# Small products of the identity between the first modulation chunks, the bias ahead of the sum, and a new order of six weight blocks

## What is computed

```python
def modulation(cond, w_mod, b_mod):
    m = jax.nn.silu(cond) @ w_mod + b_mod
    return jnp.split(m[..., None, :], 6, axis=-1)
...
    for l in range(DEPTH):
        mp = modulation(c_ctx, w_mod[l], b_mod[l])
        ms = modulation(c, w_mod[l], b_mod[l])
        hp = modulate(xp, mp[0], mp[1])
        hs = modulate(xs, ms[0], ms[1])
...
            op, ckv, kpe, kb, vb = ab_context(hp, w_in_ab[i], mla_q_norm[i], mla_w_uq[i], ...)
            os_ = ab_latent(hs, cache_mla_ckv[:, i], ...)
...
        xp = layer_norm(ALPHA * xp + mp[2] * op, ln_g[l, 0], ln_b[l, 0])
...
        fp = moe(hp, router_w, router_bias, exp_w_gate[l], exp_w_up[l], exp_w_down[l])
```

## Time and profile before

| | |
|---|---|
| median of 3 runs | 822.41 us (822.19 to 824.67) |
| the profiled execution's own time | 821.88 us |
| its span in the trace | 820.1 us |
| PE busy | 759.0 us (93% of the span) |
| DMA moved | 287.46 MB, 351 GB/s over the span |
| mean granted clock of TensorE | 0.977 |

### The profile page before, as it was taken

The page is one execution under the profiler, slowest core; times in us unless marked ns, Lnnn a source line. Parts: engine busy times, 40 slices in busy tenths (PEclk is TensorE's granted clock), DMA queues, the critical chain, the costliest instruction groups (busy, mean ns, idle before and its releaser), DMA issues.

```text
span 820.1 us, 9612 instructions
## 1 busy us (share of the span) xinstructions
PE 759.0 (93%) x3769; PEld 361.2 (44%) x3769; DVE 237.2 (29%) x550; ACT 150.9 (18%) x390; POOL 59.7 (7%) x116
## 2 busy tenths in 40 slices
PE   4799799999999999997999999999999999997894
PEld 1345444556544443443334564455544434442431
DVE  0002634447401101000418227374601010010417
ACT  0110312325011110111112132233211101110200
POOL 0000000000100010101000110000100002101000
PEclk9599999999999999999999999999999999999998
DMA  8999999915399999999999999752299999999981
GB/s 305 390 304 396 390 390 416 415 68 206 121 418 417 419 421 417 419 416 415 421 401 374 389 380 423 299 211 104 109 419 416 422 417 416 421 418 416 418 352 52
DMA packets 78530, 287.46 MB, mean 351 GB/s; under 512 B 6508, under 2 KB 12140, under 8 KB 62100
## 3 DMA queue, kind: packets, MB, share of 16 engines
q1 hardware_dynamic: 74452, 275.60, 84.9%
q10 hardware_dynamic: 2880, 7.03, 2.2%
q0 software_dynamic: 1152, 4.19, 1.3%
HBM read 278.99 MB, written 7.82 MB: 350 GB/s over the span
## 4 chain that ended last, share of the span: by engine, by line
PE 56%; SPq 23%; DMA 9%; DVE 8%; ACT 3%; issue 2%; POOL 0%; DVEq 0%; ACTq 0%
PE bank L1094 13%; SPq L600 12%; PE bank L1128 7%; DMA ring<-in_exp_w_down 6%; SPq L595 6%; PE bank L932 6%; PE bank L789 5%; PE bank L769 4%; SPq L596 4%; PE bank L1065 3%; DMA ring<-in_w_mod 2%; PE bank L878 2%; PE bank L671 2%; PE bank L720 2%; PE bank L820 2%
## 5 line engine op out<-in xcount | busy, mean ns | idle before, releaser
L1094 PE MATMUL bank<-ring,arena 128*64 128x512 f32 x1024 | 227.6, 600 | 11.3 <-DMA ring<-in_exp_w_up 10.5
L1094 PEld LDWEIGHTS bank<-ring,arena 128*64 128x64 f32 x1024 | 75.2, 138 | 160.3 <-issue 148.8
L1128 PE MATMUL bank<-ring,arena 128*64 128x512 f32 x512 | 114.3, 596 | 6.0 <-DMA ring<-in_exp_w_down 4.9
L1679 DVE TENSOR_TENSOR arena<-bank,arena 128x256 f32<-128x256 f32 x32 | 13.6, 424 | 231.5 <-ACT arena L1848 231.5
L1128 PEld LDWEIGHTS bank<-ring,arena 128*64 128x64 f32 x512 | 35.8, 137 | 72.7 <-issue 63.6
L1065 PE MATMUL bank<-arena 128*128 128x128 f32 x512 | 62.1, 275 | 0.0
L1065 PEld LDWEIGHTS bank<-arena 128*128 128x128 f32 x512 | 59.7, 192 | 1.0 <-issue 0.5
L1758 ACT ACTIVATE arena<-bank 128x512 f32<-128x512 f32 (+6 forms) x67 | 37.2, 579 | 107.6 <-PE bank L789 34.0
L1848 ACT ACTIVATE arena<-bank 128x256 f32<-128x256 f32 x32 | 12.3, 383 | 225.7 <-PE bank L1094 225.7
L1695 DVE COPY arena<-bank 128x512 f32<-128x512 f32 x14 | 9.7, 691 | 118.7 <-PE bank L1128 118.7
L789 PE MATMUL bank<-ring,arena 128*128 128x256 f32 (+1 forms) x128 | 41.6, 486 | 0.0
(11 more groups left out here) (182 smaller groups left out, 679.6 us busy)
## 6 DMA issues: line engine op xcount, KB each, us to landing
ring<-in_exp_w_gate SPq DMA_DIRECT2D x64, 1024.0 KB, 19.8
ring<-in_exp_w_up SPq DMA_DIRECT2D x64, 1024.0 KB, 19.6
ring<-in_exp_w_down SPq DMA_DIRECT2D x64, 1024.0 KB, 23.7
ring<-in_w_mod SPq DMA_DIRECT2D x24, 2048.0 KB, 19.8
expert_rows<-arena ACTq DMA_DIRECT2D x12, 512.0 KB, 7.9
ring<-in_w_out_ab SPq DMA_DIRECT2D x2, 2048.0 KB, 19.2
ring<-in_w_in_c SPq DMA_DIRECT2D x2, 2048.0 KB, 23.2
ring<-in_w_out_c SPq DMA_DIRECT2D x2, 2048.0 KB, 12.0
```

The costliest lines, as they stand in the source:

```text
L1094: mm = nc.tensor.matmul(pb(key)[SLOTS * hf:SLOTS * (hf + 1), :], xeT[b][:, k * P + SLOTS * a:k * P + SLOTS * (a + 1)], w[:, :, k % 4, hf * ...
L1128: mm = nc.tensor.matmul(pb(key)[SLOTS * a:SLOTS * (a + 1), :], hp[:, c:c + SLOTS], w[:, a, kf % 2, hf * HALF:(hf + 1) * HALF], start=(kf = ...
```

## The change

Four edits. First, ahead of the wait for each of the chunks 0 to 3, PE makes ten products of the 128 x 128 identity with itself (`stir`), into a bank that the next transposes use later. Second, in piece 0 the product with the bias comes ahead of the chunks and starts the sum. Third, both pieces are closed by a product with zeros that is two columns wide and not 512. Fourth, the order of six blocks changes from `wout 1, lora, 8, 9, 10, 11` to `8, 9, lora, wout 1, 10, 11`, and qa0 gets a wait for `lora` of its own.

```diff
--- before.py
+++ after.py
@@ -105,8 +105,9 @@
 def plan_blocks():
 
     order = [("mod", 0, c) for c in MOD_PIECES[0]] + [("win", 0, b) for b in range(3)]
-    order += [("mod", 0, c) for c in MOD_PIECES[1]] + [("wout", 0, 1), ("lora", 0, 0)]
-    order += [("mod", 0, c) for c in MOD_PIECES[2]] + [("wout", 0, 0)] + [("mod", 1, c) for c in MOD_PIECES[0]]
+    order += [("mod", 0, c) for c in MOD_PIECES[1]] + [("mod", 0, c) for c in (8, 9)]
+    order += [("lora", 0, 0), ("wout", 0, 1)] + [("mod", 0, c) for c in (10, 11)]
+    order += [("wout", 0, 0)] + [("mod", 1, c) for c in MOD_PIECES[0]]
     order += expert_blocks(0)
     order += [("win", 1, b) for b in range(len(WIN[1]))] + [("mod", 1, c) for p in (1, 2) for c in MOD_PIECES[p]]
     order += [("wout", 1, b) for b in range(2)]
@@ -677,29 +678,40 @@
             def ln_row(key, l, s, which, hf):
                 bcast(key, cst(C_ID + LN_ROW + 8 * which + 2 * (2 * l + s) + hf, 1), rows[:])
 
-            def modulation(l, piece, used=()):
-
-                key = ("mod", l, piece)
+            def modulation(piece, used=()):
+
+                key = ("mod", 0, piece)
                 room(pe, key)
                 chunks = MOD_PIECES[piece]
                 out = pb(key)
+                few = DEPTH * N_MOD
+                if piece == 0:
+                    nc.tensor.matmul(out[0:32, :], cst(C_BIAS, 32, few), rows[0:few, :],
+                                     start=True, stop=False, skip_group_check=True)
                 for c in chunks:
-                    n = index[("mod", l, c)]
+                    n = index[("mod", 0, c)]
+                    if piece == 0:
+                        stir(("hT", 0, 0, 0, 0), 10)
                     pe.wait_ge(*got(n))
                     w = block_ap(n)
                     for k in range(KD):
                         j = k % 4
                         mm = nc.tensor.matmul(out[32 * j:32 * j + 32, :], cwin[:, k, 24 - 2 * c:56 - 2 * c],
                                               w[:, k * HALF:(k + 1) * HALF],
-                                              start=(c == chunks[0] and k < 4), stop=False, skip_group_check=True)
+                                              start=(c == chunks[0] and k < 4 and (piece > 0 or k > 0)), stop=False,
+                                              skip_group_check=True)
                         if c == chunks[0] and k < len(used):
                             mm.then_inc(*release(used[k]))
                     mm.then_inc(*release(n))
-
-                bias = cst(C_BIAS + 32 * l, 32, DEPTH * N_MOD) if piece == 0 else \
-                    tri[0:DEPTH * N_MOD, 0:1].to_broadcast([DEPTH * N_MOD, 32])
-                nc.tensor.matmul(out[0:32, :], bias, rows[0:DEPTH * N_MOD, :],
+                nothing = tri[0:few, 0:1].to_broadcast([few, 32])
+                nc.tensor.matmul(out[0:32, 0:2], nothing, rows[0:few, 0:2],
                                  start=False, stop=True, skip_group_check=True).then_inc(*fill(key))
+
+            def stir(key, n):
+
+                room(pe, key)
+                for _ in range(n):
+                    nc.tensor.matmul(pb(key)[:, 0:P], ident, ident, start=True, stop=True, skip_group_check=True)
 
             def turn_rows(key, src, c0, n):
 
@@ -954,6 +966,7 @@
             def mla_queries(key):
                 g, quad = key[1] // 2, key[1] % 2
                 room(pe, key)
+                pe.wait_ge(*got(lora_n))
                 for c in range(2):
                     mm = nc.tensor.matmul(pb(key)[:, 0:4 * QK_A], qlatT[:, g, c, :],
                                           uq[:, c, 4 * quad * QK_A:4 * (quad + 1) * QK_A],
@@ -1267,13 +1280,13 @@
                     pe.wait_ge(s_const, 16)
                     turn_rows(("lnT",), rows, C_ID + LN_ROW, 16)
                     pe.wait_ge(s_cwin, 1)
-                    modulation(0, 0)
+                    modulation(0)
                     pe.wait_ge(*saved(("mod", 0, 0)))
                     mod_columns(0, 0)
                 modulated(l, 0)
                 if l == 0:
                     project(0)
-                    modulation(0, 1, (index[("win", 0, len(WIN[0]) - 1)],))
+                    modulation(1, (index[("win", 0, len(WIN[0]) - 1)],))
                 else:
                     project_odd()
                 attention(l)
```

## The result

The changed kernel takes 824.46 us (median of 20 runs, 822.5 to 828.25) against 822.12 (20 runs, 820.86 to 825.17): ratio 1.0025, 95% interval 1.0013 to 1.0036, or 1.1 to 3.0 us slower. That lies inside the range of the prediction, and under the 0.3% that it called too small to tell; 20 runs on each side do tell it. The profiled execution took 823.70, its span is 821.9: 1.8 us more than before. So the question is where a lead of several microseconds went, and what took two more.

What follows compares the result with a forecast made beforehand. PE's nearly unbroken chain from chunk 3 to the gather, then expert transfers, was taken to bound the kernel. A 0.6 us gain left at me1 and 1.75 lost to half clock gave +1.15: 823.5 median, range 820.9 to 825.5.

Steps and rivals of the forecast that it cites:

- The clock at the start: Start to projection: first stir at half speed ends by 14.6, full speed from there; projection at 36.1, 4.7 us earlier.
- The lead at the scores: First scores: PE 7.3 us ahead, 6.5 saved by the projection's first products and 0.8 more through the second closing product.
- full clock from 15 on: Sign expected in the new profile: full clock from about 15, then granted clock 0.50 for 3.4 us or more from about 102.
- The new order lets me0 pass: At me0: chunks 8 and 9 land at 76.1 and 81.5, me0 starts at about 82.2, so no wait.
- The pin on chunk 11: At me1: chunk 11 still lands at 102.2, Y0 begins at 104.3 instead of 104.9; 0.6 of 7.3 us left.
- Half speed behind the wait: From chunk 11 in me1: clock at half after gaps of 2.9 and 3.7 us; 1.75 us lost, 3.5 if rise just missed.
- The sum: Whole kernel: -0.6 + 1.75 = +1.15 us, giving 823.0 on the profiled execution and 823.5 as median.
- the clock stayed full behind the wait: Rival at me1: pin on chunk 11, but clock full or risen again when it lands; -0.6 us, 821.8; chance 0.26.
- the lead surviving: Rival at me1: chunks 10 and 11 come earlier or the wait is hidden; 815.1 whole, 818.8 half; chance 0.07.
- the clock was at full by 15.0: Answers the rival at the start that stirs don't lift the clock: first modulation ends at 42.8, 830; chance 0.04.

## Why the prediction was right

By its own steps:

- **The clock at the start.** Said: the first stir at half, ending at 14.6 at the latest, full speed from there, the projection at 36.1. Measured: 13.7, full from 15, 36.5 (in two other executions of kernels with the same start the clock fell once more for 3.4 us at 37, and the projection's first products were at half after all). Right.
- **The lead at the scores.** Said 7.3, measured 6.8; the 0.5 that is missing is chunk 3, which landed at 28.94 and not at 28.50. But here a sign of the prediction failed, full clock from 15 on: the clock fell at 79.8 behind the wait for the normalised rows, which I had taken to stay full because the kernel before stayed full over such a stretch (81.8 to 85.3 in the earlier trace rows). Scores and me0 took 3.06 and 4.89, against 1.68 and 3.83; the wait for DVE ahead of V0, 0.89 and not 2.14, gave part of it back, and the lead was 5.7 at me1. The fall cost nothing in the end, since PE had to wait in me1 anyway.
- **The new order lets me0 pass.** Right: no wait in me0; with the old order both of its chunks are waited for.
- **The pin on chunk 11.** Said: lands at 102.2, 0.6 us left. Measured 102.9 and 102.7, nothing left. The mechanism was right and the term too high: the landing of this chunk lay between 101.8 and 103.4 over the profiles in which it has this place in the stream, and in the kernel before it lay at 102.2 twice. Most of this spread is there already at chunk 3, which landed between 28.5 and 29.4; from there to chunk 11 it took 73.1 to 74.1 in all of them. In the changed kernel 0.44 of the 0.7 was there at chunk 3. Chunk 3 came at 28.50 to 28.97 in the five profiles without the products at the start and at 28.67 to 29.38 in the nine with them; whether they have a part in that is open. That the landing holds PE is shown by the order with `wout` 1 last, which moves the wait to Y0, and by the later me1: once the wait has other work in its place, the time is 5.5 us (3.4 to 7.6) under that of the kernel before.
- **Half speed behind the wait.** Said: fallen before chunk 11 comes, 1.75 us lost (1.7 to 3.5). Measured: it fell 0.8 us after the chunk had begun, 3.4 us long, 1.7 lost; in the second profile 0.7 after, 3.4 long. With ten products ahead of the chunk the fall in me1 is gone, and no loss in time is left that could be told from nothing.
- **The sum.** Said +1.15; measured +1.8 in the span and 1.1 to 3.0 in the ratio. The 0.65 between is the 0.6 that wasn't left, so the right range owes something to its width: the gain of 0.6 hung on a landing that differs by more than that from one execution to the next. The rule of the Trainium skill that I weighed (TensorE: Matmul & The Clock Gate, "HAM oscillation": bursts of products shorter than the waits for transfers between them each start at the slow clock) made the fall in me1 certain. Both profiles of the changed kernel show a fall there, though not at the start of the burst: chunk 11 ran at full for its first 0.8 and 0.7 us. The profile with the filler has none in me1.

The rivals: the clock stayed full behind the wait in neither of the two profiles of the changed kernel; the lead surviving needed an edit that the change didn't have; the clock was at full by 15.0 in all nine profiles of a kernel with the stirs. The bias ahead of the sum and the narrow closing product have no run of their own; their parts are read from the rows only (0.22 for 1.91 and 1.04).

## What to carry to other kernels

A lead that an engine wins ahead of a saturated stream of transfers is worth only the slack of the next block in it: add up the bytes ahead of each block, compare its landing with the new time at which it is wanted, and move the work that wants the late block behind work whose blocks are already there (here Y0, V1 and S3; with that the change was 5.5 us faster than the kernel before and not 2.0 slower). A lead that turns into a wait on TensorE can cost more than nothing, since the work behind the wait may start at half clock. Filler can keep the clock up, but it must be shorter than the wait in every execution, not in the one that was profiled.

## What the runs showed of the hardware

- The same kernel's clock rises and falls at other points from execution to execution. The kernel before stayed at full over 81.8 to 85.3 with PE at work for 2.10 of 3.5 us, and in its second profile fell at 83.2 after 2.43 of 3.8 us. Stretches at half elsewhere (201 to 205 in one, 575 to 578 in the other) cost 1.2 and 1.4 us: from Y0 to the gather it took 104.0 us with the one at 201 and 102.8 without, and between the last blocks of the two layers' experts 344.2 with the one at 575 and 342.8 without. One profile can't tell whether a stretch is safe, and differences under 1.5 us between two profiles are best read step by step.
- A full PE is no sign that the clock holds. In the kernel before it fell at 201.3, behind 3.4 us in which PE worked throughout, on the routing's products of 16 columns (L1038) and, in the last 0.7 us, on transposes (L753); columns as in the earlier trace rows:

```profile
197.90:201.30 3.40, 3.40 (x32) 3.40 (x32) 3.30 (x7) 0.61 (x3) 0.00 (x0) 1.00 0.22 89
201.30:204.70 3.40, 3.40 (x13) 2.46 (x12) 2.98 (x16) 3.40 (x4) 0.00 (x0) 0.50 0.00 0
```

- A long stretch at half costs what is not hidden by waits behind it: 10.3 us at half moved Y0 by 0.4 in the second profile of the kernel before, with a start 2.1 us faster, and 10.2 us moved it by 3.1 in the first profile of the order alone, with a start 0.5 slower.
